# A two-layer diffusion backbone on one core: x's rows in eight turns ahead of the slot products, the first down matrix issued in the routing stage, the last item's down products ahead of the next up products, the last up matrices in two halves

## The chip, the cores and the metric

The kernel runs on one core of a Trainium2 chip. The metric is the device time of one execution in microseconds (us). Engines: TensorE (PE, its weight loads PEld), VectorE (DVE), ScalarE (ACT), GpSimd (POOL) and SyncE (SP), which here only issues transfers.

## What is computed

Two layers over 1024 latent and 256 context tokens of width 1024. Each layer has a mixer and then a mixture of experts; layer 1 keeps only the latent tokens at its end. Only the mixture matters here:

```python
w = p_sel * p_top / jnp.sum(p_top, axis=-1, keepdims=True)
e_idx = g_idx * EXPERTS_PER_GROUP + e_local            # two of 32 experts per token
return expert_dispatch(h, e_idx, w.astype(h.dtype), w1, w3, w2)
...
def run_block(args):
    xb, e = args
    return (jax.nn.silu(xb @ w1[e]) * (xb @ w3[e])) @ w2[e]
```

Each expert has two up matrices w1 and w3 (1024 x 512) and a down matrix w2 (512 x 1024), float32, 2 MB each: 6 MB for an expert, 192 MB for a layer, and every expert of both layers is read.

## The kernel before, in words

**Two stages make a mixture.** `route` computes the router's logits, the choice of experts, and for each slot the token that lies in it (`indices`, the slot products, L1759). `experts` then runs over the slots. Each stage is a block: its engines run their own programs side by side, and none starts the next block before all have ended this one.

**Routing.** While DVE works out slots, PE turns the normalised rows (`hT`) and ACT writes them to DRAM as `h_tokens`. In layer 1 PE also turns the rows of x itself, in 16 turns of four 128x128 transposes (`first_rows_pe`, L1769); ACT copies two turns into one of four row buffers (`HROWS`) and writes 0.5 MB to `out` (`first_rows_act`); from the fifth row tile on, ACT first waits for the write that left the same buffer. `FIRST_BEFORE = 12` of these turns stand ahead of the slot products, the other four behind them, and after them `rows_of_slots` (L1790), whose result DVE copies as `slot_w`. In layer 0 there are no such turns; behind the slot products PE runs four matmuls on constants that nobody reads (`keep_running`, L253, called with 4). When the index is there, POOL gathers the first 128 rows by it (`gather_rows`, L1657).

**Weight transfers.** All are issued by SP, each of 2 MB. There are three places each for up matrices (`w13`) and down matrices (`w2`), and expert j uses place j modulo 3 (`RING`). SP issues w13 of expert 0 in `route` (L1649, called from `load_up`). w2 of expert 0 is issued only in `experts` (L1653, called from `load_down`), behind a wait for the gather. After it come w13 of 1, w13 of 2, w2 of 1, w13 of 3, w2 of 2 and so on; w13 of j waits until the up products of expert j-3 have ended, w2 of j until its down products have. The last four are w13 of 31 (both matrices), w2 of 30, w2 of 31.

**Items.** PE takes the slots in items. Layer 1 has 42 items of 64 slots, numbered 0 to 41. An item is 64 up matmuls (`up_pair`, L2192), SiLU on ACT, a product on DVE (L2443), four transposes (L2265), a copy on DVE (`g_out`, L2453) and 32 down matmuls (`down_pair`, L2229). PE's order is: transposes of item i, up products of i+1, down products of i. So SiLU and product of i+1 run beneath the down products of i. Item 41 alone belongs to expert 31, item 40 alone to expert 30, item 39 to 29. `y_gated` (L2461) weighs the result of an item on DVE and POOL adds it to `out` (L2152). In layer 0 some items are of 128 slots and computed with split numbers (L2200 to L2206), and ACT and DVE make the split halves of the weights.

Of the kernel before, what the change touches and what calls it, by code (L numbers as in the profile page):

```python
# [14 lines left out]
P = 128  # L15
D = 1024
KT = D // P
# [200 lines left out]
class Program:  # L218
# [1380 lines left out]
    def experts_open(self, ctx, layer, nt):  # L1599
# [38 lines left out]
        if layer == DEPTH - 1:  # L1638
            N = len(work_items(layer))
            ring["to_row"] = self.sb(ctx, "to_row", [PAIR, 3, N], I32)  # L1640
            ring["slot_w"] = self.sb(ctx, "slot_w", [P, N])
            ring["s_first"] = [self.sem(ctx, f"e_first{i}") for i in range(HROWS)]
        ring["s_w13"], ring["s_w2"] = ([self.sem(ctx, f"e_{n}{c}") for c in range(RING)] for n in ("w13", "w2"))
        return ring

    def load_up(self, sp, layer, ring, j, e):
        for m, name in enumerate(("exp_w1", "exp_w3")):
            src = self.i[name][layer, bass.ds(e, 1), :, :].rearrange("a (p k) n -> p (a k) n", p=P)
            sp.dma_start(ring["w13"][j % RING][:, m, :, :], src).then_inc(ring["s_w13"][j % RING], 16)  # L1649
# [14 lines left out]
    def route(self, layer, nt, ring):  # L1664
# [3 lines left out]
        with ExitStack() as ctx:  # L1668
# [36 lines left out]
            ADA_BEHIND = {3: 0, 6: 1, 9: 2}  # L1705
            FIRST_BEFORE = 12
            COUNTS_BEFORE = 9 if nt > LT else 10
# [7 lines left out]
            def _(sp):  # L1715
# [9 lines left out]
                sp.wait_ge(s_te, 2 * nt)  # L1725
                self.load_up(sp, layer, ring, 0, first)
                for i in range(HROWS):
                    sp.wait_ge(s_hw[i], 16 * len(range(i, nt, HROWS)))
# [93 lines left out]
            def _(pe):  # L1822
# [43 lines left out]
                if closing:  # L1866
                    for n in range(FIRST_BEFORE, 2 * nt):
                        first_rows_pe(pe, n)
                    rows_of_slots(pe)
                else:  # L1870
                    self.keep_running(pe, tr[0][:], 4)

# [135 lines left out]
    def experts(self, layer, nt, ring):  # L2008
# [20 lines left out]
        with ExitStack() as ctx:  # L2029
# [55 lines left out]
            def _(sp):  # L2085
                sp.wait_ge(s_x[0], 16)
                self.load_down(sp, layer, ring, 0, self.expert_of(sp, layer, 0))
                def down_of(j, e):
# [82 lines left out]
            def _(pe):  # L2171
# [12 lines left out]
                def up_pair(i):  # L2184
                    q, u, _ = items[i]
                    pe.wait_ge(s_xt, q + 1)
                    arrived(s_w13, i, 32)
                    for k in range(KT):
                        for half in range(2):
                            for n in range(2):  # L2190
                                row, at = half * PAIR + n * UNIT, u % 4 * UNIT + n * UNIT
                                ins = pe.matmul(ph[row:row + UNIT, :], xt[:, k, at:at + UNIT],  # L2192
                                                w13[place[u + n] % RING][:, half, k, :], start=(k == 0), stop=(k == KT - 1))
                    ins.then_inc(s_a, 1)
# [64 lines left out]
                for i in range(N):  # L2259
                    pe.wait_ge(s_g, i + 1)  # L2260
                    for k in range(FT):
                        if full[i]:
                            ins = pe.transpose(pg[:, k * P:(k + 1) * P], hid[:, k * P:(k + 1) * P], self.c("ident"))
                        else:
                            ins = pe.transpose(pg[:, k * PAIR:(k + 1) * PAIR], hid[PAIR:P, k * P:(k + 1) * P],  # L2265
                                               self.const[PAIR:P, COL["ident"] + PAIR:COL["ident"] + P])
                    ins.then_inc(s_gt, 1)
                    if i + 1 < N:
                        up(i + 1)
                        if ends_quad[i + 1] and items[i + 1][0] + 1 < NQUAD:  # L2270
                            transpose_x(items[i + 1][0] + 1)
                    down(i)

# [140 lines left out]
            def _(dve):  # L2414
# [56 lines left out]
                for i in range(-1, N):  # L2471
                    if i + 1 < N and full[i + 1]:
                        x_low(i + 1)
                        low(i + 1, range(0, HI_RING))
                    if gated and i >= 1:
                        y_gated(i - 1)
                    if i >= 0:
                        g_out(i)
                        if full[i]:
                            low(i, range(KT, KT + FT))  # L2480
                    if i + 1 < N:
                        if full[i + 1]:
# [604 lines left out]
```

## Time and profile before

| | |
|---|---|
| time, median of 3 runs | 2327.96 us (2326.31 to 2332.64) |
| the profiled execution's own time | 2324.93 us |
| its span | 2323.1 us |
| PE busy | 2154.0 us (93%) |
| DVE, ACT, POOL busy | 990.0 us (43%), 765.5 us (33%), 237.4 us (10%) |
| moved by DMA | 587.42 MB, mean 253 GB/s |
| experts of layer 0, of layer 1 | about 751 to 1303 us, 1770 to 2317 us |

The span goes from the first to the last instruction that the profiler saw; the execution's own time is 1.8 us longer. Busy shares are means over stages of very different kinds, so they say little on an edit at one place; what counts is which wait ends last there.

### The profile page before, as it was taken

To read this page: it belongs to the slowest core of one execution; us is meant where nothing else is said; L and a number is where in the kernel's file an instruction comes from. 1 tells how busy PE (TensorE), PEld (TensorE's weight loads), DVE (VectorE), ACT (ScalarE), POOL (GpSimd) and SP (SyncE) were. 2 spreads that over 40 slices of the span, in tenths; PEclk is the share of its full clock that TensorE was granted. 3 is DMA by queue.
4 is the path that set the end of the run, shared out by engine and by line. 5 is a ranking of instruction groups with operands and counts; after the bars stand their busy time and mean duration, and the time that the engine had idled before them with its cause. 6 is when DMAs were issued, how large, how long until landed. Compare 5 with 4: busy or idle time off the path is not lost. (4 is left out here: it accounts for less than half of the span.)

```text
span 2323.1 us, 33794 instructions
## 1 busy us (share of the span) xinstructions
PE 2154.0 (93%) x14214; PEld 1206.2 (52%) x14214; DVE 990.0 (43%) x1511; ACT 765.5 (33%) x1163; POOL 237.4 (10%) x160
## 2 busy tenths in 40 slices
PE   7999989989997999999999889998988999998977
PEld 5788876546674555455555444444854333322322
DVE  7333326656335545445454453666443222222211
ACT  5411006544224444434444256564232010100100
POOL 0010000000000000000000303550000111111110
PEclk9999999999999999999999999999997999999989
DMA  9201108016717999999999701003139999999996
GB/s 357 60 28 37 37 33 338 1 53 244 256 27 266 425 426 427 426 427 426 426 426 419 274 31 36 23 13 145 37 130 373 402 399 404 405 415 414 414 408 225
DMA packets 142572, 587.42 MB, mean 253 GB/s; under 512 B 25972, under 2 KB 62544, under 8 KB 117456
## 3 DMA queue, kind: packets, MB, share of 16 engines
q1 hardware_dynamic: 116672, 516.47, 55.2%
q0 software_dynamic: 13568, 40.91, 5.5%
q10 hardware_dynamic: 12176, 27.81, 3.2%
q8 instruction: 116, 1.90, 0.3%
q14 instruction: 40, 0.33, 0.0%
HBM read 529.05 MB, written 63.18 MB: 255 GB/s over the span
## 5 line engine op out<-in xcount | busy, mean ns | idle before, releaser
L2192 PE MATMUL ph<-w,x_t 128*32 128x512 f32 x4352 | 494.7, 607 | 38.6 <-DMA w<-in_exp_w 37.5
L2192 PEld LDWEIGHTS ph<-w,x_t 128*32 128x32 f32 x4352 | 141.3, 112 | 337.3 <-issue 333.0
L2229 PE MATMUL py<-w,g_t 128*32 128x512 f32 x2176 | 248.8, 598 | 7.2 <-DMA w<-in_exp_w 5.0
L2443 DVE TENSOR_TENSOR hidden<-hidden,ph 64x512 f32<-64x512 f32 x68 | 73.7, 1084 | 406.8 <-ACT hidden L2358 405.9
L2358 ACT ACTIVATE hidden<-ph 64x512 f32<-64x512 f32 x68 | 40.2, 592 | 577.0 <-PE ph L2192 577.0
L2434 DVE TENSOR_TENSOR w_low<-w,w_high 128x1024 fp32r<-128x1024 f32 x156 | 180.6, 1219 | 15.1 <-ACT w_high L2344 15.0
L2740 PE MATMUL z<-hT,w_cd 128*128 128x512 f32 (+1 forms) x448 | 184.4, 569 | 0.0
L811 PE MATMUL z<-h_high,w_hi 128*128 128x512 f32 (+1 forms) x432 | 159.4, 369 | 3.9 <-DVE h_low L906 3.5
L2344 ACT ACTIVATE w_high<-w 128x1024 fp32r<-128x1024 f32 x156 | 152.2, 1048 | 21.6 <-PE ph L2202 14.3
L812 PE MATMUL z<-h_low,w_hi 128*128 128x512 f32 (+1 forms) x432 | 155.8, 361 | 0.0
L813 PE MATMUL z<-h_high,w_lo 128*128 128x512 f32 (+1 forms) x432 | 155.6, 360 | 0.0
L1657 POOL DMA_INDIRECT x_rows<-h_tokens,index x37 | 37.5, 1012 | 1106.9 <-DVE index L1994 558.2
L2229 PEld LDWEIGHTS py<-w,g_t 128*32 128x32 f32 x2176 | 67.5, 110 | 150.5 <-issue 148.0
L2740 PEld LDWEIGHTS z<-hT,w_cd 128*128 128x128 f32 x448 | 85.3, 192 | 90.7 <-issue 88.7
L1453 PE MATMUL z<-Y_high,w_o_hi 128*128 128x512 f32 (+1 forms) x320 | 121.9, 381 | 4.7 <-DVE xT L1525 2.6
L1454 PE MATMUL z<-Y_low,w_o_hi 128*128 128x512 f32 (+1 forms) x320 | 119.1, 372 | 0.0
L1455 PE MATMUL z<-Y_high,w_o_lo 128*128 128x512 f32 (+1 forms) x320 | 119.1, 372 | 0.0
L811 PEld LDWEIGHTS z<-h_high,w_hi 128*128 128x128 f32 x432 | 83.4, 193 | 21.6 <-DVE h_low L906 6.2
L813 PEld LDWEIGHTS z<-h_high,w_lo 128*128 128x128 f32 x432 | 83.2, 193 | 12.1
L812 PEld LDWEIGHTS z<-h_low,w_hi 128*128 128x128 f32 x432 | 83.0, 192 | 12.2 <-issue 1.2
L2152 POOL DMA_INDIRECT out<-xT,to_row x37 | 52.1, 1407 | 310.7 <-DMA out<-xT,to_row 128.2
L1158 DVE CUSTOM_DVE_ANT_0 scores<-s_pair,band,minus_sink 128x640 f32<-128x640 f32 (+1 forms) x80 | 61.1, 801 | 45.2 <-PE s_pair L1084 45.1
(388 smaller groups left out, 3071.1 us busy)
## 6 DMA issues: line engine op xcount, KB each, us to landing
w<-in_exp_w SPq DMA_DIRECT2D x192, 2048.0 KB, 23.8
ada_raw<-in_ada_w SPq DMA_DIRECT2D x16, 2048.0 KB, 8.7
y_slots<-zero SPq DMA_DIRECT2D x29, 512.0 KB, 15.0
w<-in_ada_w SPq DMA_DIRECT2D x5, 2048.0 KB, 13.0
h_tokens<-h_rows ACTq DMA_DIRECT2D x18, 512.0 KB, 2.7
w_ab<-in_w_in_ab SPq DMA_DIRECT2D x14, 512.0 KB, 3.8
y_slots<-y_rows ACTq DMA_DIRECT2D x26, 256.0 KB, 10.8
y_slots<-y_rows ACTq DMA_DIRECT2D x52, 128.0 KB, 9.2
```

The costliest lines, as they stand in the source:

```text
L811: pe.matmul(z[n % 2][:, 0:size], w_hi[:, m % 2, k, :], h_hi, start=(k == 0), stop=False)
L812: pe.matmul(z[n % 2][:, 0:size], w_hi[:, m % 2, k, :], h_lo, start=False, stop=False)
L813: ins = pe.matmul(z[n % 2][:, 0:size], w_lo[:, m % 2, k, :], h_hi, start=False, stop=(k == KT - 1))
L1453: pe.matmul(out, w_hi[:, k, slot(m)], Y_hi[:, k, own[c]], start=(k == 0), stop=False)
L1454: pe.matmul(out, w_hi[:, k, slot(m)], self.Y_lo[:, k, own[c]], start=False, stop=False)
L1455: ins = pe.matmul(out, w_lo[:, k, slot(m)], Y_hi[:, k, own[c]], start=False, stop=(k == 2 * BR - 1))
L2192: ins = pe.matmul(ph[row:row + UNIT, :], xt[:, k, at:at + UNIT], w13[place[u + n] % RING][:, half, k, :], start=(k == 0), stop=(k == KT - 1))
L2229: ins = pe.matmul(py[bufs[i][0]][row:row + UNIT, :], gt[:, k, n * UNIT:(n + 1) * UNIT], w2[place[u + n] % RING][:, k, half * 512:(half + 1 ...
L2344: act.activation(self.w_high[:, c % HI_RING, :].rearrange("p (a n) -> p a n", a=2), src, ACT.Copy).then_inc(s_hi, 1)
L2434: dve.tensor_tensor(low_part, whole, self.w_high[:, c % HI_RING, :].rearrange("p (a n) -> p a n", a=2).bitcast(F32), ALU.subtract).then_in ...
L2443: dve.tensor_tensor(hid[PAIR:P, :].rearrange("s (k q) -> s q k", k=FT), hid[0:PAIR, :].rearrange("s (q k) -> s q k", k=FT), ph[PAIR:P, :]. ...
L2740: ins = pe.matmul(z[n % 2][:, 0:size], w[:, m % NW, k, :], hT[:, k, at:at + size], start=(k == 0), stop=(k == KT - 1))
```

## The change

There are five edits. (1) `FIRST_BEFORE` goes from 12 to 8: the slot products of layer 1 stand behind eight turns, and eight turns come after them. (2) w2 of expert 0 is issued in `route`, behind w13 of expert 0 and behind a wait for products that have read the place's earlier content; in `experts` the wait for the gather and this transfer are gone. Both layers have this. (3) In layer 0 `keep_running` after the slot products has two matmuls instead of four. (4) In layer 1 the down products of item 40 stand ahead of the up products of item 41, and DVE's `y_gated` of item 40 stands behind its `g_out`. (5) w13 of expert 31 in layer 1 is loaded as four transfers of 1 MB, first the lower half of both matrices' rows and then the upper, which has a semaphore of its own that PE waits for in the middle of the up products.

```diff
+            ring["s_half"] = self.sem(ctx, "e_half")
...
     def load_up(self, sp, layer, ring, j, e):
+        if layer == DEPTH - 1 and j == NE - 1:
+            for ks, sem in ((slice(0, KT // 2), ring["s_w13"][j % RING]), (slice(KT // 2, KT), ring["s_half"])):
+                for m, name in enumerate(("exp_w1", "exp_w3")):
+                    src = self.i[name][layer, bass.ds(e, 1), :, :].rearrange("a (p k) n -> p (a k) n", p=P)
+                    sp.dma_start(ring["w13"][j % RING][:, m, ks, :], src[:, ks, :]).then_inc(sem, 16)
+            return
...
-            FIRST_BEFORE = 12
+            FIRST_BEFORE = 8
...
                 self.load_up(sp, layer, ring, 0, first)
+                if NA:
+                    sp.wait_ge(ada["used"], NA)
+                self.load_down(sp, layer, ring, 0, first)
...
-                    self.keep_running(pe, tr[0][:], 4)
+                    self.keep_running(pe, tr[0][:], 2)
...
             def _(sp):
-                sp.wait_ge(s_x[0], 16)
-                self.load_down(sp, layer, ring, 0, self.expert_of(sp, layer, 0))
...
                     for k in range(KT):
+                        if gated and k == KT // 2 and NE - 1 in place[u:u + 2]:
+                            pe.wait_ge(ring["s_half"], 32)
...
+                    down_first = gated and i + 2 == N
+                    if down_first:
+                        down(i)
                     if i + 1 < N:
                         up(i + 1)
...
-                    down(i)
+                    if not down_first:
+                        down(i)
...
-                    if gated and i >= 1:
+                    if gated and 1 <= i < N - 1:
                         y_gated(i - 1)
...
+                    if gated and i == N - 2:
+                        y_gated(N - 2)
```

SP at the passage from `route` to `experts` in layer 0, before (w_0, w_1, w_2 are places, of `w13` in rows of L1649 and of `w2` in rows of L1653; the branches end and begin a block):

```order
L1649 DMA w_0<-in_exp_w 128x4096 x2
L1668 UNCONDITIONAL_BRANCH
L2084 UNCONDITIONAL_BRANCH
L1662 TENSOR_LOAD table
L1662 ISA x2
L1653 ISA
L1653 DMA w_0<-in_exp_w 128x4096
```

The same place after the change (L1656 loads up matrices, L1660 down matrices):

```order
L1656 DMA w_0<-in_exp_w 128x4096 x2
L1660 DMA w_0<-in_exp_w 128x4096
L1675 UNCONDITIONAL_BRANCH
L2094 UNCONDITIONAL_BRANCH
L1669 TENSOR_LOAD table
L1669 ISA x2
L1656 ISA
L1656 DMA w_1<-in_exp_w 128x4096 x2
```

The down matrix of expert 0 has moved over the block's edge, and the first transfer of the new block is that of expert 1's up matrices.

SP at the end of layer 1 after the change (in these names w_1_2 with x2 is expert 31's place for up matrices, then w_0_2 and w_1_2 are the down places of experts 30 and 31):

```order
L1652 ISA
L1652 DMA w_1_2<-in_exp_w 128x2048 x2
L1652 ISA
L1652 DMA w_1_2<-in_exp_w 128x2048 x2
L1660 DMA w_0_2<-in_exp_w 128x4096
L1660 DMA w_1_2<-in_exp_w 128x4096
```

Two transfers have become four, and the order of the matrices is what it was: w2 of 30 still stands behind all of w13 of 31.

PE at the end of layer 1, before (L2192 up products, L2229 down products, L2265 transposes of the hidden rows):

```order
L2265 MATMUL pg<-const,hidden 128x64 x4
L2192 MATMUL ph<-w_0_2,x_t 32x512 x32
L2229 MATMUL py_2<-w_2_2,g_t 32x512 x16
L2265 MATMUL pg<-const,hidden 128x64 x4
L2192 MATMUL ph<-w_1_2,x_t 32x512 x32
L2229 MATMUL py_2<-w_0_2,g_t 32x512 x16
```

And after (the same lines, now L2275, L2202 and L2239):

```order
L2275 MATMUL pg<-const,hidden 128x64 x4
L2202 MATMUL ph<-w_0_2,x_t 32x512 x32
L2239 MATMUL py_2<-w_2_2,g_t 32x512 x16
L2275 MATMUL pg<-const,hidden 128x64 x4
L2239 MATMUL py_2<-w_0_2,g_t 32x512 x16
L2202 MATMUL ph<-w_1_2,x_t 32x512 x32
```

The products with w2 of expert 30 (w_0_2, g_t) now stand ahead of the products with w13 of expert 31 (w_1_2, x_t).

## Rows read from the trace of the kernel before

**Rows 1.** Engines by stretch: us, PE busy, ..., clock, DMA share, GB/s
```profile
1780.00:2010.00 230.00, 228.16 (x2068) 74.17 (x2064) 58.91 (x79) 22.67 (x31) 38.73 (x30) 0.99 1.01 404
2010.00:2290.00 280.00, 244.24 (x2108) 81.09 (x2100) 62.87 (x84) 22.09 (x30) 45.55 (x35) 0.95 1.01 412
```

**Rows 2.** Waits of PE from 750 to 1300 us, and its timeline there
```profile
PE ph L2192 <- DMA w<-in_exp_w: 4.3, 3, 2.4
...
951.84 7.07 PE L2192 MATMUL ph<-w,x_t 128*32 128x512 f32 x64 [2.40 <-DMA w<-in_exp_w]
```

**Rows 3.** Timeline of SP's queue at layer 0's passage: start, us
```profile
731.05 0.86 SPq L1649 DMA_DIRECT2D w<-in_exp_w  x2
752.13 0.34 SPq L1653 DMA_DIRECT2D w<-in_exp_w  x1
```

**Rows 4.** Timeline of PE at the same place
```profile
743.55 0.64 PE L1759 MATMUL bc<-in_unit,at_place 128*32 128x26 f32 x29 [3.85 <-issue]
...
745.96 5.18 PE L253 MATMUL tr<-const 128*128 128x512 f32 x8
751.44 1.06 PE L2176 MATMUL px<-const,x_rows 128*128 128x128 f32 x8 [0.30 <-PEq L1668]
```

**Rows 5.** Gathers (L1657) issued at 745.9 and at 753.3 us
```profile
DMA to landing us min/median/max: 4.6/4.6/4.6
...
DMA to landing us min/median/max: 11.5/11.5/11.5
```

**Rows 6.** Timeline of SP's queue at layer 1's passage
```profile
1743.51 0.84 SPq L1649 DMA_DIRECT2D w<-in_exp_w  x2
1771.34 0.34 SPq L1653 DMA_DIRECT2D w<-in_exp_w  x1
```

**Rows 7.** Timelines of PE and ACT at layer 1's passage
```profile
1757.30 1.12 PE L1769 MATMUL tr<-const,xT 128*128 128x128 f32 x4 [3.89 <-ACT h_rows L1781]
...
1759.20 1.92 PE L1759 MATMUL bc<-in_unit,at_place 128*32 128x21 f32 x128
...
1767.30 2.44 PE L1790 MATMUL pr<-in_unit,weighed 128*32 128x42 f32 x128
...
1759.99 0.60 ACT L1781 ACTIVATE h_rows<-tr 128x512 f32<-128x512 f32 x1 [2.26 <-DMA out<-h_rows]
```

**Rows 8.** Landing of weight transfers issued at 1771.3, 915.4 and 2009.3 us
```profile
DMA to landing us min/median/max: 8.5/8.5/8.5
...
DMA to landing us min/median/max: 13.8/16.2/18.6
...
DMA to landing us min/median/max: 9.9/12.7/15.6
```

**Rows 9.** Chain, SP's queue, landings from 2253.3 to 2257 and of 2274.1
```profile
2253.79 38.45 DMA w<-in_exp_w
...
2256.64 17.79 SPq L1653 DMA_DIRECT2D w<-in_exp_w  x2
...
DMA to landing us min/median/max: 27.8/38.4/41.9
...
DMA to landing us min/median/max: 29.1/29.1/29.1
```

**Rows 10.** Timeline of PE at the end
```profile
2283.40 3.64 PE L2229 MATMUL py<-w,g_t 128*32 128x512 f32 x32
...
2292.37 8.47 PE L2192 MATMUL ph<-w,x_t 128*32 128x512 f32 x64 [4.94 <-DMA w<-in_exp_w]
...
2304.20 0.46 PE L2265 MATMUL pg<-const,hidden 64*128 64x64 f32 x4
2306.36 3.64 PE L2229 MATMUL py<-w,g_t 128*32 128x512 f32 x32 [1.69 <-DVE g_t L2453]
```

**Rows 11.** Timeline of DVE at the end
```profile
2301.53 1.08 DVE L2443 TENSOR_TENSOR hidden<-hidden,ph 64x512 f32<-64x512 f32 x1 [12.45 <-ACT hidden L2358]
...
2305.88 0.42 DVE L2453 COPY g_t<-pg 128x256 f32<-128x256 f32 x1
```

## The prediction

> **What bounds the kernel now.** I read the page first, then the engines by stretch, the chain that ended last, the waits, and SP's queue with the landing of each transfer. In the experts of both layers the DMA engines are never idle, but that does not say who leads. From 1780 to 2010 us PE is busy 228 of 230 us, and from 2010 to 2290 only 244 of 280 [rows 1]. The landings tell the two apart: a 2 MB weight transfer that finds its queue empty lands 8.5 us after its issue. At 2009.3 us, when PE has freed a place, the first one lands after 9.9 us [rows 8], so at most 1.4 us of older work was queued. Up to there PE leads: a transfer starts when PE frees its place. From there on the queue grows: at the end a transfer needs 38 to 42 us [rows 9]. The last ten experts of layer 1 have two units of slots each, so each item asks for a whole expert's 6 MB, and DMA leads. In layer 0 PE leads too, with three waits for weights, 4.3 us in all, the longest 2.40 us [rows 2].
>
> So an edit ahead of the experts moves the time by what it moves PE's first item and removes of later waits. An edit at the end is worth what it does to the chain behind the last landings.
>
> **Layer 0, w2 of expert 0 issued early.** Its issue goes from 752.13 us to right behind w13 of expert 0, issued at 731.05 [rows 3]. The place's earlier reader has ended by then: its products stand ahead of the index. The first transfer of the new block is then w13 of expert 1, one transfer (about 5 us, half of the 10 us by which a pair's data follow each other) earlier in the stream. Since SP's wait for the gather is gone and the block starts some 2 us earlier (below), the stream is up to 8 us ahead of before. Later requests are tied to PE, and at 915.4 us a transfer landed after 13.8 us against 8.5 alone [rows 8]: 5.3 us of old work was queued. So about 5 us of the lead survives that point, more than the longest wait of 2.40 us. I take all three waits as gone: **-4.3 us**. The bounds are 0 (if PE's own delay eats them) and -4.3.
>
> **Layer 0, two dummies less, no wait for the gather.** Eight rows (four matmuls of two passes) take 5.18 us from 745.96 and end at 751.14; PE starts the block's first transposes at 751.44, 0.30 us after the barrier [rows 4]. Half of them end at 748.6, so the block could start at 748.9. But the gather, issued at 745.9, lands after 4.6 us, at 750.5 [rows 5]. Now w2 of expert 0 is in flight until about 749, and a gather that shares the engines with weights took 11.5 us [rows 5]. My value: its first 1.5 us of data run against weights, the rest free, so it lands near 752 and PE starts **0.6 us later** than before. The bounds: it lands as before, -0.9 us; it takes the full 11.5 us and lands at 757.4, +6.0 us. PE's sequencer also stood still for 3.85 us without a partner while w13 of expert 0 was loading [rows 4]; a second such stop under the added transfer lies within these bounds.
>
> The two dummies are also there for the clock. The Trainium skill (TensorE: Matmul & The Clock Gate, "The HAM clock gate") says that an idle array falls to half its clock and gets it back only after sustained work, and so speaks against taking them out. By the rule the first item would run longer at half clock; at the price that such a return has elsewhere in the trace (8.47 against 7.07 us for the same 64 up matmuls [rows 2, 10]) the whole would come out 1.4 us above my sum. I leave it out, since PE waits ahead of that item in both kernels.
>
> **Layer 1, eight turns instead of twelve.** Before, PE waits 3.89 us in front of turn 8, because ACT waits for a row buffer's write to `out`, and the slot products start only at 1759.20 [rows 7]. Now they fill that wait: `in_unit` is ready at about 1752.5 (PE's 8 turns end at 1752), so they start some 6.6 us earlier. The eight turns behind them are paced by the same writes: the buffer of row tile 5 is free at 1759.99 [rows 7], and w2 of expert 0, now in flight beside them, delays the next two. I estimate that `rows_of_slots` starts at 1765.6 instead of 1767.30 and the block ends **1.6 us earlier**. The bounds are -3.5 us (all the waiting filled, no contention) and +1 (the gather, now issued near 1756.6 among the loads, lands after some 15 us instead of 11.5). w2 of expert 0 leaves 1771.34 for 1744.4 [rows 6], but from 1780 PE leads, so its 5 us of stream are worth only the small backlog at the place where DMA takes over: at most 1.4 us [rows 8], I take **0.6**.
>
> **The end of layer 1.** This is the largest term. PE ends item 39 at 2287.0 and its transposes at 2287.5, and waits until 2292.37, when w13 of expert 31 has landed: the chain has the transfer issued at 2253.79 land after 38.45 us, at 2292.2 [rows 9, 10]. w2 of expert 30 is issued behind it, at 2256.64, and lands after 41.9 us, at **2298.5** [rows 9]. Before, this hurts nobody: PE needs it only after up products of 8.47 us, at 2300.8. After the change PE needs it first. So item 40's down products cannot fill the wait, the wait becomes 11 us instead of 4.94, and the halves of w13 of 31 are of no use, since both have long landed when PE comes to them. From 2298.6: down products 3.64, return of the clock 1.40, up products 7.07, together 2310.7. SiLU then takes 0.69 (from 2300.84 to DVE's start at 2301.53), the product 1.08, the transposes 0.46, the copy 0.42, with 0.15 between them [rows 10, 11]; before, SiLU and product ran beneath the down products. The last down products start at 2313.5 instead of 2306.36: **+7.1 us**. w2 of 31 is issued at 2274.1 and lands after 29.1 us, at 2303.2, in time [rows 9]. What follows (`y_gated`, the add, the close) is unchanged. The bounds: +6 (the clock's return costs nothing more than before) and +9 (twice as much, and the four smaller transfers cost 0.5 us). The moved `y_gated` of item 40 lies under the up products.
>
> **Sum.** -4.3 +0.6 -1.6 -0.6 +7.1 = +1.2 us. On the profiled execution (2324.93 us, span 2323.1) this gives 2326.1; the median of the three runs is 3.0 us above it, so 2327.96 + 1.2 = **2329.2 us**. A measurement of this kernel tells about 0.3%, 7 us, from no change.
>
> **The rivals.**
> *A, no measurable change (my forecast):* starts give up to 6 us, the end takes 7. From the ends of the bounds that belong together: -4.3 -0.9 -3.5 -1.4 +6 = -4.1, and 0 +2 +1 0 +7.1 = about +10, of which I hold the middle part likely: 2324 to 2335. 70 in 100.
> *B, slower, by the gathers:* SP's wait was what kept weights out of the gather's way. If layer 0's gather shares the engines throughout, it lands at 757.4 and PE starts 6.0 us later; layer 1's eats the 1.6 us. Then +6.0 -4.3 -0.6 +7.1 = +8.2, 2336 us, and with the end at +9, 2338. For it speaks that 11.5 us was measured under load, against it that w2 of expert 0 has nearly landed when the gather begins. It decides once the gather lands after 755 us. The Trainium skill (DMA: Bandwidth & Descriptors, "Queues, rings and completion order") has each DMA engine take turns between the queues that have work, which is this rival's mechanism. 18 in 100.
> *C, faster, by the order of landing:* if w2 of 30 lands before PE has ended item 39, its down products fill the wait, the up products start on the first half, and 2292.4 is followed by half of them (3.5), 2.8 of exposed steps and the last down products at 2298.7: -7.7 at the end, 2314 in all. Against it: SP issues w2 of 30 last, and it landed 6.3 us after w13 of 31. For it only that DMAs of one queue need not land in order. 6 in 100.
> *D, the starts give nothing:* PE's first items stay where they were and the waits in layer 0 come back elsewhere, as each later request is tied to PE. Then +7.1 alone: 2335 us, on the border. 6 in 100, split between same and slower.
>
> **How the numbers follow.** Faster: C, and a tail of A: 9. Same: most of A and half of D: 70. Slower: B, half of D: 21. The range reaches from the good end of A to B: 2323 to 2337. For A alone it is 2324 to 2335.
>
> **What would show it.** Down products of item 40 that start just after their matrix lands, near 2298 less the shift, behind a wait of some 11 us put down to a weight transfer; the last down products start about 15 us behind that landing; no wait for the upper half of w13 of 31. At the head of layer 0, PE's first transposes between 750.5 and 753 us and no wait for weights of over 1 us between 760 and 1250. At the head of layer 1 a slot product near 1752.6 less layer 0's shift, and the first up product 1 to 3 us earlier against the start of its routing. I am wrong if w2 of 30 lands ahead of w13 of 31's end, or if a gather takes over 8 us in layer 0.

## The result and the profile after

The changed kernel takes 2336.75 us, the median of 7 runs (2326.04 to 2340.19), against 2328.37 us of the kernel before in its 7 runs: ratio 1.0038, with an interval of 1.0021 to 1.0056. By the ratio it is some 9 us (5 to 13) slower, where 1.2 us were forecast. A second set of runs gave 1.0035 (1.0021 to 1.0049).

The profiled execution hides this: 2326.04 us with a span of 2324.1 us, 1.0 us over that of before. In it the first expert transfer of layer 0 is issued at 725.52 us, in before at 731.05 [rows 3], although nothing ahead of that place was changed. Over the 14 profiles of this study the place lies anywhere between 725.5 and 735.2 us. So stretches between marks inside the program are compared below, not spans.

**The engines by stretch**, of the changed kernel (columns as in [rows 1]):

```profile
1780.00:2010.00 230.00, 229.53 (x2096) 75.03 (x2100) 60.39 (x81) 22.09 (x30) 38.73 (x30) 1.00 1.00 398
2010.00:2290.00 280.00, 243.94 (x2076) 79.97 (x2068) 60.86 (x82) 22.09 (x30) 46.36 (x35) 0.93 1.01 411
```

PE still leads up to 2010 us and the DMA engines from there. The waits of PE in layer 0's experts (750 to 1300 us), those of 2010 to 2300 us, and the gather issued at 740.8 us:

```profile
PE ph L2202 <- DMA w<-in_exp_w: 1.6, 1, 1.6
...
PE ph L2202 <- DMA w<-in_exp_w: 23.1, 7, 4.7
PE py L2239 <- DMA w<-in_exp_w: 15.8, 3, 9.1
...
DMA to landing us min/median/max: 5.3/5.3/5.3
```

Three waits for weights in layer 0 [rows 2] have become one of 1.6 us. The gather lands after 5.3 us, 0.7 us later than in before and far from 11.5 [rows 5].

**PE at layer 0's passage**, of the changed kernel:

```profile
738.51 0.64 PE L1769 MATMUL bc<-in_unit,at_place 128*32 128x26 f32 x29 [4.33 <-issue]
...
740.92 3.76 PE L253 MATMUL tr<-const 128*128 128x512 f32 x4
746.52 1.94 PE L2184 MATMUL px<-const,x_rows 128*128 128x128 f32 x8 [1.84 <-PEq L1675]
...
755.28 1.05 PE L2216 MATMUL ph<-w_low,x_high 128*128 128x512 f32 x2
756.14 0.86 PE L2210 MATMUL ph<-w_high,x_high 128*128 128x512 f32 x2
756.83 0.62 PE L2212 MATMUL ph<-w_high,x_low 128*128 128x512 f32 x2
```

The block's first transposes stand 21.00 us behind the first transfer, 20.39 in before [rows 3, 4]. In before they follow the dummies, in the changed kernel they stand 1.84 us behind the dummies' end, just after the gather has landed (746.1). But then the first item runs slower: a pair of matmuls takes 1.05 us up to 756.1 and 0.62 from 756.8.

**ACT and PE at layer 1's passage**, whose first transfer is issued at 1737.36 us, and the landings of ACT's writes to `out` issued at 1742.84, 1744.40 and 1745.96:

```profile
1759.07 0.60 ACT L1791 ACTIVATE h_rows<-tr 128x512 f32<-128x512 f32 x1 [5.81 <-DMA out<-h_rows]
...
1763.04 0.60 ACT L1791 ACTIVATE h_rows<-tr 128x512 f32<-128x512 f32 x1 [2.88 <-DMA out<-h_rows]
...
1746.48 1.92 PE L1769 MATMUL bc<-in_unit,at_place 128*32 128x21 f32 x128 [1.40 <-DVE in_unit L1988]
...
1759.72 1.11 PE L1779 MATMUL tr<-const,xT 128*128 128x128 f32 x4 [4.93 <-ACT h_rows L1791]
...
1765.59 2.05 PE L1800 MATMUL pr<-in_unit,weighed 128*32 128x42 f32 x128
...
1771.56 3.64 PE L2202 MATMUL ph<-w,x_t 128*32 128x512 f32 x32 [1.11 <-ACT x_t L2343]
...
DMA to landing us min/median/max: 16.1/16.1/16.1
...
DMA to landing us min/median/max: 18.6/18.6/18.6
...
DMA to landing us min/median/max: 18.2/18.2/18.2
```

In before the same three landed after 10.9, 10.7 and 11.0 us. Counted from the first transfer, the slot products start at 9.12 us instead of 15.69 [rows 6, 7], as forecast. The wait that they were to fill has not gone, it has moved behind them and grown: ACT waits 5.81 and 2.88 us for row buffers (3.96 and 2.26 in before), and PE with it. `rows_of_slots` starts at 28.23 us instead of 23.79, and the first up product stands at 34.20. In before that product is at 30.16 (1773.67 less 1743.51).

**The end**, of the changed kernel: SP's queue, the landings of w13 of 31 (four transfers), of w2 of 30 and of w2 of 31, then PE and DVE:

```profile
2249.16 1.81 SPq L1652 DMA_DIRECT2D w<-in_exp_w  x4
2252.44 16.43 SPq L1660 DMA_DIRECT2D w<-in_exp_w  x2
...
DMA to landing us min/median/max: 25.0/31.2/36.3
...
DMA to landing us min/median/max: 40.3/40.3/40.3
...
DMA to landing us min/median/max: 29.3/29.3/29.3
...
2283.22 0.46 PE L2275 MATMUL pg<-const,hidden 64*128 64x64 f32 x4
2292.83 5.20 PE L2239 MATMUL py<-w,g_t 128*32 128x512 f32 x32 [9.15 <-DMA w<-in_exp_w]
2297.84 7.05 PE L2202 MATMUL ph<-w,x_t 128*32 128x512 f32 x64
2306.67 0.46 PE L2275 MATMUL pg<-const,hidden 64*128 64x64 f32 x4 [1.77 <-DVE hidden L2457]
2307.64 3.64 PE L2239 MATMUL py<-w,g_t 128*32 128x512 f32 x32 [0.52 <-DVE g_t L2467]
...
2305.59 1.02 DVE L2457 TENSOR_TENSOR hidden<-hidden,ph 64x512 f32<-64x512 f32 x1 [5.97 <-ACT hidden L2372]
```

This is the picture that was forecast. w13 of 31 has landed by 2286.9 (2250.6 for the last issue, and 36.3 us at most), w2 of 30 lands at 2292.7, and PE, which now wants w2 of 30 first, waits 9.15 us for it with the up products standing behind. From there to the last down products it is 14.8 us (15 forecast).

**Stretches.** T0 and T1 are the issues of the first expert transfer in layer 0 and 1, "next px" the transposes behind the first item of layer 0, "end 0" its last down products, "U1" the first up product of layer 1, "E" DVE's last instruction. Every number is a difference of two starts in the timelines.

```
us              T0 to   next px    T0 to   end 0   T1 to   U1 to   T1 to
kernel          next px to end 0   end 0   to T1   U1      E       E
before          36.57   526.24     562.81  449.65  30.16   543.40  573.56
before_again    36.59   527.46     564.05  447.98  29.97   542.94  572.91
after           39.03   523.26     562.29  449.55  34.20   546.53  580.73
after_again     37.48   523.28     560.76  448.29  34.05   546.51  580.56
late_l1         39.05   525.19     564.24  448.03  27.42   549.90  577.32
swap            37.71   523.31     561.02  448.03  34.11   539.80  573.91
tail_back       39.07   523.31     562.38  452.20  34.51   539.80  574.31
turns12         39.09   523.31     562.40  452.42  31.84   546.50  578.34
l0_back         36.78   527.43     564.21  451.10  34.14   546.75  580.89
best            36.94   523.79     560.73  448.08  27.44   542.81  570.25
turns8_only     36.51   527.64     564.15  451.19  27.41   543.37  570.78
dummies4        37.13   523.27     560.40  448.80  33.99   546.35  580.34
halves_only     36.34   526.07     562.41  450.06  28.29   541.72  570.01
mid_w2          36.96   524.12     561.08  453.31  27.98   540.51  568.49
```

The two executions of one text (before, after) differ by up to 1.7 us in a stretch, and the stretch between the layers' experts, which no kernel here changes, takes 448.0 to 453.3 us. Layer 1 holds the loss: T1 to E is 7.4 us longer (mean of two each, 580.65 less 573.24), of which 4.1 us lie ahead of the first up product. Layer 0 is 1.9 us shorter (T0 to end 0, 561.5 less 563.4).

### The profile page after: what moved, and what is told of

Same layout as the page of the kernel before. It is cut to its first block and busy times, and to the rows that moved or that the text cites. A ratio compares the mean times of both kernels' runs of the same rounds, so it can differ in the third digit from the quotient of the medians.

```text
span 2324.1 us, 33783 instructions
## 1 busy us (share of the span) xinstructions
PE 2148.1 (92%) x14210; PEld 1198.9 (52%) x14210; DVE 990.3 (43%) x1511; ACT 765.1 (33%) x1163; POOL 237.4 (10%) x160
## 5 line engine op out<-in xcount | busy, mean ns | idle before, releaser
L2202 PE MATMUL ph<-w,x_t 128*32 128x512 f32 x4352 | 493.8, 606 | 25.7 <-DMA w<-in_exp_w 24.6
L2202 PEld LDWEIGHTS ph<-w,x_t 128*32 128x32 f32 x4352 | 139.5, 112 | 325.5 <-issue 321.2
L2239 PE MATMUL py<-w,g_t 128*32 128x512 f32 x2176 | 251.8, 604 | 16.9 <-DMA w<-in_exp_w 15.8
L2239 PEld LDWEIGHTS py<-w,g_t 128*32 128x32 f32 x2176 | 67.7, 111 | 162.0 <-issue 160.7
```

What stands on the lines that cost most here:

```text
L2239: ins = pe.matmul(py[bufs[i][0]][row:row + UNIT, :], gt[:, k, n * UNIT:(n + 1) * UNIT], w2[place[u + n] % RING][:, k, half * 512:(half + 1 ...
```

## The experiments

The theory after the result: (1) at the end the new order costs some 7 us; (2) at the head of layer 1 the early w2 makes ACT's writes to `out` land late, which costs more than the eight turns give; (3) in layer 0 the early w2 gives some 3 us, and two dummies less take part of it back through the clock. The rivals: at the head the eight turns do the harm, not w2; at the end the four smaller transfers do it, not the order; layer 0's edits do the harm.

### The kernels again

**after_again** and **before_again** are the two texts unchanged, for the spread.

> The changed kernel once more, for its spread. In its first profile the passage from routing to experts of layer 0 came 5.5 us earlier than in the kernel before (first expert transfer at 725.5 against 731.1 us) although no instruction ahead of it differs. Theory: that lead is chance, and the change costs about 6.5 us behind that point, so this profile has layer 1's head (first expert transfer to first up matmul) at 34 us again, the stretch from there to the last DVE instruction at 546 to 547 us, and the time is 2330 to 2338 us. Rival: the lead belongs to the change; then it shows again at 725 to 726 us.

> The kernel before, as a run of its own. Theory: the stretches are properties of the program, only the place of the first expert transfer of layer 0 drifts by chance (731.1, 725.5, 730.6, 731.1, 735.2, 727.4 us in six profiles): from that transfer to PE's first transposes 20.4 us, from layer 1's first expert transfer to its first up matmul 30.2 us, from there to the last DVE instruction 543.4 us, the ratio within 0.2% of 1. Rival: one of the stretches drifts by 3 us or more as well, and differences of that size between single profiles say nothing.

Measured: 2331.51 us, 1.0035 (1.0021 to 1.0049), and 2324.2 us, 1.0005 (0.9989 to 1.0022). So the loss comes back, and two sets of runs of one text differ by 0.05% here. One forecast stretch of before_again missed: its first transposes in layer 0 stand 21.9 us behind T0 instead of 20.4, while the next px is back at 36.59. Its four dummies, at the same place, take longer than the 5.18 us of before [rows 4]:

```profile
746.77 6.42 PE L253 MATMUL tr<-const 128*128 128x512 f32 x8
```

What PE loses in the dummies it gains in the first item behind them, so the place of the first transposes alone says little.

### w2 of layer 1 late again: late_l1

```diff
                 self.load_up(sp, layer, ring, 0, first)
-                if NA:
+                if not closing:
                     sp.wait_ge(ada["used"], NA)
-                self.load_down(sp, layer, ring, 0, first)
+                    self.load_down(sp, layer, ring, 0, first)
...
             def _(sp):
+                if gated:
+                    sp.wait_ge(s_x[0], 16)
+                    self.load_down(sp, layer, ring, 0, self.expert_of(sp, layer, 0))
```

> The changed kernel, but w2 of expert 0 in layer 1 alone is issued in the experts' block behind the gather, as before the change. Theory (the early transfer shares the engines with the writes to out, whose landing rose from 11 to 18 us, and ACT waits for their buffers): layer 1's head falls from 34.2 to 27 to 29 us, below the 30.2 of the kernel before, since the slot products then fill the wait; the time falls by 4 to 6 us. Rival (eight turns behind the slot products are the cause): the head stays at 33 to 34 us and the time within 1 us.

Measured: 2329.02 us, 1.0011 (0.9999 to 1.0023). T1 to U1 falls from 34.1 to 27.42 us. In its trace, `rows_of_slots` and the first up product, its first transfer being issued at 1743.34, and the landings of the same three writes:

```profile
1765.09 1.76 PE L1800 MATMUL pr<-in_unit,weighed 128*32 128x42 f32 x128
...
1770.76 4.50 PE L2205 MATMUL ph<-w,x_t 128*32 128x512 f32 x40 [1.11 <-ACT x_t L2346]
...
DMA to landing us min/median/max: 11.8/11.8/11.8
...
DMA to landing us min/median/max: 11.4/11.4/11.4
```

(The second and the fourth write both take 11.8 us, the third 11.4.) Theory 2 holds: without w2 beside them the writes land after 11 to 12 us instead of 16 to 19, and the eight turns alone bring the head 2.7 us below before's 30.1, more than the 1.6 us forecast. The stream pays part back, since U1 to E grows from 546.5 to 549.9. Over the whole layer w2 in its early place costs 3.3 us (580.65 less 577.32), less than the 4 to 6 us expected of the time.

### Twelve turns with w2 early: turns12

```diff
-            FIRST_BEFORE = 8
+            FIRST_BEFORE = 12
```

> The changed kernel, but with twelve turns ahead of the slot products. Theory (the early transfer delays the writes to out, and ACT's wait for their buffers then stands ahead of turns 8 to 11 and so of the slot products): layer 1's head is 36 to 38 us, 2 to 4 us longer than the changed kernel's 34.1, as the slot products no longer fill the wait. Rival (the turns' new place is what made the head longer): the head comes back to 30 us.

Measured: 2330.27 us, 1.0024 (1.001 to 1.0039); T1 to U1 is 31.84 us, below after's 34.1 and not above it. ACT's waits for row buffers and the landing of the second to fourth write in its trace:

```profile
1757.83 0.60 ACT L1791 ACTIVATE h_rows<-tr 128x512 f32<-128x512 f32 x1 [4.58 <-DMA out<-h_rows]
...
1765.46 0.60 ACT L1791 ACTIVATE h_rows<-tr 128x512 f32<-128x512 f32 x1 [6.54 <-DMA out<-h_rows]
...
DMA to landing us min/median/max: 15.5/15.5/15.5
...
DMA to landing us min/median/max: 16.0/16.0/16.0
...
DMA to landing us min/median/max: 15.7/15.7/15.7
```

I had expected the eight turns to help here as well, and they don't. With late w2 they are worth -2.5 us over T1 to E (turns8_only, below), with early w2 they cost 2.3 us (580.65 against 578.34). From the other side, w2's early place costs 3.3 us beside eight turns. Beside twelve it gives about 1.4 us: turns12 takes 5.1 us more than before over T1 to E (578.34 less 573.24), and 6.5 of them are the end's, by late_l1 less turns8_only, which differ in layer 1 by the end's edits alone (577.32 less 570.78). The two edits clash. What differs in the traces: with eight turns the gather of the first item goes out at 1750.4 us, 13.0 us behind the first transfer, while w2 and the writes are still on the engines, and the third and fourth write land some 2.5 us later than with twelve turns. That the gather is what delays them is argued from this, not tried by itself, and stays open.

### Eight turns alone: turns8_only

The kernel before, with one number changed:

```diff
-            FIRST_BEFORE = 12
+            FIRST_BEFORE = 8
```

> The kernel before with eight turns instead of twelve ahead of the slot products, and nothing else. Theory: head of layer 1 (first expert transfer to first up matmul) 27.4 us against 30.1, layer 1's later course shifted with it, as DMA leads at the end and its requests shift too: time 2 to 3 us below the kernel before. Rival (DMA's bandwidth sets the end from layer 1's first transfer on): the head gains, the stretch behind it gives it back, time within 1 us of before.

Measured: 2320.33 us, 0.9984 (0.9963 to 1.0005); T1 to U1 is 27.41 us and T1 to E 570.78, 2.5 us less than before. The rival that the eight turns do the harm falls: alone they gain some 2.5 us by the stretches. The time's interval takes in no change.

### The end: tail_back and swap

**tail_back** puts the down products of item 40 behind the up products again and keeps the halves; **swap** keeps PE's new order and issues w2 of 30 ahead of w13 of 31.

```diff
-                    down_first = gated and i + 2 == N
+                    down_first = False
...
-                    if gated and 1 <= i < N - 1:
+                    if gated and i >= 1:
                         y_gated(i - 1)
...
-                    if gated and i == N - 2:
-                        y_gated(N - 2)
```

```diff
                     e = self.expert_of(sp, layer, j)
+                    if gated and j == NE - 1:
+                        down_of(j - 1, upper)
                     if j >= RING:
                         sp.wait_ge(s_a, last[j - RING] + 1)
                     self.load_up(sp, layer, ring, j, e)
-                    if j > 1:
+                    if j > 1 and not (gated and j == NE - 1):
                         down_of(j - 1, upper)
```

> The changed kernel with the order of PE and DVE for items 40 and 41 as before, w13 of 31 still in halves. Theory: from the first up product of layer 1 to the last down products it is 6 to 7 us less than in the changed kernel (536.1 us), so 529 to 530, and the half loads are worth up to 3 us more, as the up products start when the lower half is there. Rival: the tail's order does nothing and the changed kernel's loss lies at the heads; then 535 to 537 us.

> The changed kernel, but at the end of layer 1 SP issues w2 of expert 30 ahead of w13 of expert 31. Theory (item 40's down products wait for a matrix that lands last): the wait of 9.2 us ahead of them is gone, they run in the wait for w13 of 31, the up products of item 41 start on the lower half with a wait for the upper in their middle, and the last down products start some 10 us earlier against the first up product of the layer (536.1 us in the changed kernel, 532.7 before). Rival (the slowest DMA engine sets all last landings, so the order is worth little): less than 4 us.

Measured: tail_back 2323.89 us, 1.0007 (0.9989 to 1.0025); swap 2323.08 us, 0.9988 (0.9977 to 0.9998). In both U1 to E is 539.80 us, 6.7 us less than in after. PE in tail_back:

```profile
2289.93 0.46 PE L2275 MATMUL pg<-const,hidden 64*128 64x64 f32 x4
2290.32 7.33 PE L2202 MATMUL ph<-w,x_t 128*32 128x512 f32 x64
2299.84 3.64 PE L2239 MATMUL py<-w,g_t 128*32 128x512 f32 x32 [2.19 <-DMA w<-in_exp_w]
```

And PE in swap:

```profile
2290.23 0.46 PE L2277 MATMUL pg<-const,hidden 64*128 64x64 f32 x4
2292.38 5.34 PE L2241 MATMUL py<-w,g_t 128*32 128x512 f32 x32 [1.69 <-DVE g_t L2469]
2297.53 7.05 PE L2204 MATMUL ph<-w,x_t 128*32 128x512 f32 x64
```

In tail_back the up products start without a wait and w2 of 30 costs 2.19 us; in swap w2 of 30 is there when PE wants it (PE waits for `g_t` alone) and the up products follow at once. Counted from U1, swap's last down products start 7.1 us earlier than in after (529.0 against 536.1), not the 10 expected, and there is no wait for the upper half in the middle of the up products. PE's order does no harm by itself, only against the order of the transfers. Theory 1 holds, in mechanism and in size. But swap gains nothing over tail_back (both 539.80): beside the halves, the new order with the transfers swapped is worth as much as the old order.

### The halves alone: halves_only

The kernel before with the halves (the new branch of `load_up`, and PE's wait for the upper half in front of the middle `k`), and nothing else.

```diff
+        if layer == DEPTH - 1 and j == NE - 1:
+            for ks, sem in ((slice(0, KT // 2), ring["s_w13"][j % RING]), (slice(KT // 2, KT), ring["s_half"])):
...
+                        if gated and k == KT // 2 and NE - 1 in place[u:u + 2]:
+                            pe.wait_ge(ring["s_half"], 32)
```

> The kernel before with w13 of expert 31 of layer 1 in two halves, nothing else. Theory (the up products of item 41 start when the lower half is there, some 5 us before the upper, and are followed by the down products of item 40, for which w2 of 30 lands 6 us later): the last up products start some 5 us earlier, but the down products of item 40 then wait for w2 of 30, so that the end comes 1 to 3 us earlier. Rival: the first halves land with the second ones, since all four transfers queue on the slowest engine, and nothing moves.

Measured: 2324.89 us, 0.9992 (0.9976 to 1.0009). U1 to E is 541.72 us, 1.5 us less than the mean of before's two: a small gain if any, not to be told from nothing by the times. As expected the last up products start earlier (by 4.1 us, counted from U1) and w2 of 30 is then waited for (2.14 us). Its head, 28.29 us against 30.1, is shorter too, though nothing was changed there; that stays unexplained, and is a measure of how far one profile can be trusted. The rival that four smaller transfers do the harm falls.

### Layer 0: l0_back and dummies4

**l0_back** undoes layer 0's edits (w2 behind the gather again, four dummies); **dummies4** is the changed kernel with four dummies.

```diff
-                if NA:
+                if closing:
                     sp.wait_ge(ada["used"], NA)
-                self.load_down(sp, layer, ring, 0, first)
+                    self.load_down(sp, layer, ring, 0, first)
...
-                    self.keep_running(pe, tr[0][:], 2)
+                    self.keep_running(pe, tr[0][:], 4)
...
+                if not gated:
+                    sp.wait_ge(s_x[0], 16)
+                    self.load_down(sp, layer, ring, 0, self.expert_of(sp, layer, 0))
```

```diff
-                    self.keep_running(pe, tr[0][:], 2)
+                    self.keep_running(pe, tr[0][:], 4)
```

> The changed kernel with layer 0's two edits undone (w2 of expert 0 behind the gather, four dummies), the others kept. Theory (the early gather contention costs 0.6 us, half the clock's return some 1 to 2 us, and the earlier stream takes away 2.7 us of waits for weights): PE's first transposes 20.4 us after the first expert transfer instead of 21.0, 3 waits for weights of 4.3 us again, and layer 0 as a whole within 1 us of the changed kernel, so the same time as the changed kernel within 2 us. Rival (layer 0's edits gain as forecast): 3 to 4 us slower than the changed kernel.

> The changed kernel with four dummies again. Theory (two dummies leave the array at half its clock through the first item): the transposes behind the first item of layer 0 stand 36.6 to 37 us after the first expert transfer, as in the two profiles of the kernel before and in both kernels with four dummies, instead of 37.5 to 39.1 in the six with two; time 0 to 2 us below the changed kernel. Rival (these 2 us are the gather's contention with the early transfer): still 38 to 39 us.

Measured: l0_back 2336.87 us, 1.0059 (1.0041 to 1.0077), slower than the changed kernel's 1.0035; dummies4 2329.37 us, 1.0018 (0.9998 to 1.0039). So layer 0's edits together seem to help, though the intervals overlap: my own expectation, a time within 2 us of the changed kernel, missed, and the rival of 3 to 4 us came nearer. The stretches say it more clearly. The five profiles with w2 late in layer 0 need 526.97 us in the mean from the next px to end 0, the nine with w2 early 523.65: **-3.3 us**. From T0 to the next px the eight profiles with four dummies need 36.7 us in the mean, the six with two 38.6: **+1.8 us**. Of this some 0.4 us belong to w2 and not to the dummies: among the nine profiles with w2 early, three with four dummies need 37.0 us, so the dummies alone make 1.6. That holds dummies4's expectation (37.13 us), against its rival of 38 to 39. The first item of layer 0 by stretch (columns as in [rows 1]), first in after, from 751 us:

```profile
751.00:756.00 5.00, 5.00 (x12) 3.94 (x13) 5.00 (x5) 3.73 (x5) 0.00 (x0) 0.50 0.99 423
```

Then in dummies4, whose T0 is 2.55 us later, from 753.5 us:

```profile
753.50:758.50 5.00, 5.00 (x18) 4.03 (x17) 5.00 (x6) 3.91 (x5) 0.00 (x0) 0.73 0.98 417
```

PE is busy throughout in both, at a granted clock of 0.50, the lower level (1.2 GHz), in after and of 0.73 in dummies4, which does 18 matmuls in the time of 12. The Trainium skill (TensorE: Matmul & The Clock Gate, "The HAM clock gate") says that an idle array drops to half its clock and comes back only after sustained work. The traces agree, with 1.6 us as its price here.

### Two combinations: best and mid_w2

**best** is the changed kernel with the edits of late_l1, swap and dummies4: eight turns, w2 of expert 0 early in layer 0 alone, four dummies, and at the end w2 of 30 ahead of the halves of w13 of 31. **mid_w2** is swap with four dummies and, in layer 1, w2 of expert 0 issued in the routing, but only when ACT has seen its last row buffer free:

```diff
                 self.load_up(sp, layer, ring, 0, first)
-                if NA:
-                    sp.wait_ge(ada["used"], NA)
+                sp.wait_ge(ada["used"], NA)
+                if closing:
+                    sp.wait_ge(s_xe, 2 * nt - 1)
                 self.load_down(sp, layer, ring, 0, first)
```

> Eight turns; w2 of expert 0 early in layer 0 only; four dummies; item 40's down products first, with w2 of 30 issued ahead of w13 of 31, which is loaded in halves. Theory (each part's own effect adds up): head of layer 1 27.4 us, first up product to the last DVE instruction some 6.7 us below the 549.9 of the kernel with the late transfer in layer 1, so 543, and a time 5 to 8 us below the kernel before. Rival (DMA leads layer 1 from its first transfer to its last landing, so what the head gains comes back as waits): within 3 us of the version that only swapped the order, which was 2.8 us below the kernel before.

> The best kernel so far (eight turns, w2 of 30 ahead of w13 of 31, item 40's down products first, four dummies), but w2 of expert 0 in layer 1 is issued in routing, only after ACT has passed its last wait for a row buffer. Theory (the early transfer hurts only through those waits, and the end is led by DMA, so 2 MB moved into the idle stretch before the experts are worth up to 5 us there): head 27 to 28 us, the stretch from first up product to the last DVE instruction 540 instead of 542.8, time 2 to 3 us below the best. Rival (it now meets the gather's or the block's code loading): the head grows by 1 us or more and the time is that of the best or above.

Measured: best 2317.14 us, 0.9971 (0.9958 to 0.9983); mid_w2 2314.8 us, 0.9956 (0.9938 to 0.9974). In mid_w2 w2 goes out 21.9 us behind the first transfer (0.9 in after, 27.8 in before [rows 6]). The head stays at 27.98 us, and with 568.49 us from T1 to E layer 1 is 4.7 us shorter than in before. PE at the end of best:

```profile
2278.27 3.64 PE L2244 MATMUL py<-w,g_t 128*32 128x512 f32 x32 [1.69 <-DVE g_t L2472]
2281.72 3.62 PE L2207 MATMUL ph<-w,x_t 128*32 128x512 f32 x32
2287.62 5.34 PE L2207 MATMUL ph<-w,x_t 128*32 128x512 f32 x32 [2.28 <-DMA w<-in_exp_w]
2294.72 0.46 PE L2280 MATMUL pg<-const,hidden 64*128 64x64 f32 x4 [1.77 <-DVE hidden L2462]
```

Here the halves work as they are meant to: the down products of item 40, then the up products with the lower half, then 2.28 us of waiting for the upper one. Yet the whole rework of the end is worth almost nothing over the end of before: best and turns8_only differ in layer 1 by it alone, and T1 to E is 570.25 against 570.78 us. With w2 of 30 ahead, w13 of 31 comes later. In best PE can start the second half of the up products only 523.9 us after U1 (2287.62 less 1763.75), while in before it has all of w13 of 31 after 518.7 us (2292.37 less 1773.67). Both combinations beat both kernels, by the head of layer 1, by layer 0 and, in mid_w2, by w2's new place. The intervals of best and mid_w2 overlap, so which of the two is faster is not settled.

## Why the prediction was wrong

It forecast +1.2 us, and +8.8 us were timed; the profiles' stretches give about +5.5 (7.4 in layer 1, -1.9 in layer 0). The range held the time, but the case that was forecast, no measurable change, did not come.

- **The end, +7.1 us: right.** The wait ahead of item 40's down products is put down to w2 of 30 and is 9.15 us long (11 forecast). Counted from T1 that matrix lands at 555.4 us (555.0 in before), but PE comes to the wait some 2.4 us later than in before, as its head was late. The end's edits are worth 6.5 us, and undone from either side the order gives back 6.7.
- **Layer 1's head, "1.6 us earlier": wrong, and the largest miss.** The first up product came 4.1 us later. The slot products did move by the 6.6 us forecast. The step that failed is the pacing of the turns behind them, "w2 of expert 0, now in flight beside them, delays the next two", which I had put into an estimate of 1765.6 us for `rows_of_slots` (1771.7 on before's time scale was measured). I saw the contention and priced it low: between the 1.6 us taken and the 3.5 us of the bound without contention lie 1.9 us. Writes of 0.5 MB that land after 10.9 us without w2 landed after up to 18.6 us beside it. The bound of +1 us counted only the gather, not the writes, so this cost had no bound at all. That bound also started from a wrong row: 11.5 us was the landing of layer 0's second gather, while the first of layer 1 landed after 5.0 us in before. In the changed kernel that one took 12.1 us, and nothing waited for it. The trace of before had a row for the contention: a gather's landing goes from 4.6 to 11.5 us beside weights [rows 5].
- **w2 early in layer 1's stream, "0.6": mis-sized.** Over U1 to E it is worth 3.4 us (late_l1 against after), beside 6.7 us of harm to the head of eight turns (34.12 less 27.42). Judged by one landing at 2009.3 us the backlog had looked like at most 1.4 us [rows 8].
- **w2 early in layer 0, "-4.3": right in kind, -3.3 us measured.** One wait of 1.6 us is left, where none over 1 us was forecast.
- **The gather in layer 0, "0.6 us later": near, in part by luck.** It landed after 5.3 us, 0.7 later, and against T0 the transposes started 0.6 us later than in the one profile at hand. They were 0.9 us earlier than in before_again, as that place moves with the dummies. Rival B, the price of 11.5 us, did not happen there; its mechanism, a second queue on the same engines, happened in layer 1 and hit ACT's writes. The Trainium skill (DMA: Bandwidth & Descriptors, "Queues, rings and completion order") has each engine take turns between queues with work; the landings of the writes, 11 against 16 to 19 us, are in line with it.
- **The clock, left out "since PE waits ahead of that item in both kernels": wrong.** Two dummies less cost 1.6 us up to the next px. That PE waits in both kernels said nothing about how much work stood in front of the wait, and that is what was halved. The 1.4 us that the prediction worked out beside its sum would have been near.
- **Rival C** (the landing order) did not happen in after, since w2 of 30 landed last, some 6 us behind w13 of 31. Made to happen in best by swapping the transfers, it did not give the 7.7 us that it promised against before, but 0.5 (570.25 against 570.78 in turns8_only). The step that it had wrong is 2292.4 as a fixed landing of w13 of 31: with w2 of 30 ahead of it, PE got the second half 5.2 us later, and that half ran at 5.34 us instead of 3.6. **Rival D**, the starts give nothing (2335 us), is close to what came in total, though not for its reason: layer 0 gave 1.9 us, and layer 1's head took instead of giving. In **A**'s upper sum the +2 is worked out from nothing; layer 0's own upper bound was +6.0.

With the measured sizes the sum is -3.3 +1.8 in layer 0, +4.1 at the head, -3.4 in the stream and +6.5 at the end: +5.7 us. That lies in the lower part of the timed +8.8 (5 to 13); the rest of some 3 us, if there is one, shows in no stretch of the profiles and stays open.

## What to carry to other kernels

Before a load is moved into a quiet stretch, list what else is on the DMA engines there and which engine waits for it: small writes whose buffers are reused soon can pay more for a 2 MB neighbour than the load gains (6.7 against 3.4 us with eight turns here), and two edits that each help (fewer turns, an earlier load) can cost time together. If a consumer is put ahead of another against the order of their transfers, it waits for the later one: here that cost 6.5 us. Swapping the transfers too took the cost away but gained nothing beyond (0.5 us), since the matrix put behind then lands later. Ask of each such swap what it delays. Work that only keeps PE busy is priced by what runs behind the next wait.

## What the runs showed of the hardware

- The second to fourth write of 0.5 MB from ACT's queue land after 10.7 to 11.0 us with w13 of expert 0 beside them (before), 11.4 to 11.8 in late_l1, and after 16.1 to 18.6 us (after) or 15.5 to 16.0 (turns12) when 2 MB more stand on SP's queue.
- Programs that are the same up to there reach one place of layer 0 between 725.5 and 735.2 us, and a stretch of some 450 us that no kernel here changes takes 448.0 to 453.3 us. A single span can hide a loss of 9 us.
- The first item's time from its transposes to the next ones takes one of two values: 14.7 or 16.1 us with four dummies, about 16.5 or 18.1 us with two. Which one comes changes from execution to execution of the same text (before 16.2 and 14.7, after 18.0 and 16.5). With four dummies the two values go with the length of the dummies themselves: 16.1 behind dummies of 5.0 to 5.2 us (three profiles), 14.7 behind 6.3 to 6.6 us (five), and the sum of dummies and item is 21.0 to 21.4 us in all eight.
